# A hybrid diffusion step: the first expert weights in short runs, a third spare place, an output slot given back by TensorE

## What is computed

```python
h = rmsnorm(x, norm_mix[l]) * (1.0 + sc1) + sh1
y, new_lru, new_hgrn = token_mixer(h, ...)      # RG-LRU and HGRN2 scans, then y @ w_out
x = x + g1 * y
h = rmsnorm(x, norm_ffn[l]) * (1.0 + sc2) + sh2
x = x + g2 * expert_choice_ffn(h, w_router[l], w_gate[l], w_up[l], w_down[l])
y_out = rmsnorm(x, norm_final)
```

## Time and profile before

| | |
|---|---|
| median of 3 runs | 993.48 us (990.89 to 993.88) |
| the profiled execution | 991.45 us, span 989.7 us |
| TensorE busy | 946.9 us (96%) |
| DMA | 276.08 MB, 63.5% of the 16 engines' span on SyncE's queue |
| loads of expert pieces | 32 gate, 32 down, 30 up into the ring, 2 up into spare places |

### The profile page before, as it was taken

How to read it: one execution, slowest core, us unless ns; L and a number is a source line. 1 busy time by engine, 2 the same in 40 slices (tenths; PEclk the granted TensorE clock), 3 DMA queues, 4 the chain that set the end, 5 groups by cost and what they waited for, 6 DMA issues and landing times.

```text
span 989.7 us, 18270 instructions
## 1 busy us (share of the span) xinstructions
PE 946.9 (96%) x7806; PEld 412.4 (42%) x7806; DVE 479.7 (48%) x1136; ACT 304.4 (31%) x547; POOL 101.4 (10%) x112
## 2 busy tenths in 40 slices
PE   5999899999999999999899999999999999999996
PEld 4555556666666554463222222222222222223222
DVE  4577666464643663665445134451344415533155
ACT  5137756573653654333020020200200102002002
POOL 3200010000000011211101101011010110200100
PEclk9999999999999999999899999999999999999999
DMA  9990014504027641137899999999999999999992
GB/s 331 332 387 19 1 29 154 176 6 171 6 91 270 251 151 65 76 137 268 318 414 378 416 428 400 419 414 409 425 401 418 419 411 417 403 428 417 413 382 107
DMA packets 49828, 276.08 MB, mean 279 GB/s; under 512 B 4048, under 2 KB 12400, under 8 KB 37616
## 3 DMA queue, kind: packets, MB, share of 16 engines
q1 hardware_dynamic: 42432, 253.24, 63.5%
q0 software_dynamic: 5824, 16.81, 5.7%
q10 hardware_dynamic: 1520, 5.28, 1.4%
HBM read 262.30 MB, written 13.01 MB: 278 GB/s over the span
## 4 chain that ended last, share of the span: by engine, by line
PE 44%; DMA 7%; DVE 0%; issue 0%; ACT 0%; SPq 0%
PE p L626 26%; PE pa L626 17%; DMA ring<-in_w_down_dram 6%; PE pa L1197 0%; DMA reg_c<-h_rows,row_p 0%; DVE reg_a L2126 0%; DVE reg_a L2121 0%; ACT reg_d L1247 0%; SPq L479 0%; PE p L1091 0%; DVE reg_d L2131 0%; ACT stat L1247 0%; DVE stat L2125 0%
## 5 line engine op out<-in xcount | busy, mean ns | idle before, releaser
L626 PE MATMUL pa<-ring,reg_b 128*32 128x512 f32 (+1 forms) x2144 | 292.9, 596 | 1.0 <-ACT reg_b L1247 0.8
L626 PE MATMUL p<-ring,reg_b 128*16 128x512 f32 (+1 forms) x2528 | 280.6, 594 | 4.6 <-DMA ring<-in_w_down_dram 3.2
L626 PE MATMUL pa<-reg_a,ring 128*128 128x512 f32 (+1 forms) x768 | 227.1, 449 | 5.9 <-DVE reg_a L1624 3.3
L626 PEld LDWEIGHTS pa<-ring,reg_b 128*32 128x32 f32 (+1 forms) x2144 | 93.2, 116 | 179.8 <-issue 177.2
L626 PEld LDWEIGHTS pa<-reg_a,ring 128*128 128x128 f32 x768 | 118.1, 191 | 98.4 <-issue 98.3
L626 PEld LDWEIGHTS p<-ring,reg_b 128*16 128x16 f32 (+1 forms) x2528 | 76.6, 102 | 197.3 <-issue 196.6
L1247 ACT ACTIVATE reg_b<-pa 128x512 f32<-128x512 f32 (+1 forms) x28 | 17.1, 612 | 409.0 <-PE pa L626 213.4
L2044 DVE TENSOR_TENSOR reg_b<-reg_b,pa 128x512 f32<-128x512 f32 x16 | 11.0, 688 | 165.4 <-PE pa L626 165.1
L2028 DVE STREAM_TRANSPOSE reg_b<-reg_b 32x128 f32<-32x128 f32 x256 | 77.5, 303 | 3.8
L1247 ACT ACT_TABLE_LOAD x57 | 73.1, 1283 | 4.0 <-issue 2.8
L2028 DVE STREAM_TRANSPOSE reg_d<-reg_c 32x256 f32<-32x256 f32 x140 | 61.0, 436 | 8.7 <-DMA reg_c<-h_rows,row_s 6.7
(11 more groups left out here) (321 smaller groups left out, 750.9 us busy)
## 6 DMA issues: line engine op xcount, KB each, us to landing
ring<-in_w_gate_dram SPq DMA_DIRECT2D x32, 2048.0 KB, 12.8
ring<-in_w_down_dram SPq DMA_DIRECT2D x32, 2048.0 KB, 14.7
ring<-in_w_up_dram SPq DMA_DIRECT2D x30, 2048.0 KB, 14.1
ring<-in_w_ada_dram SPq DMA_DIRECT2D x8, 2048.0 KB
ring<-in_w_in_dram SPq DMA_DIRECT2D x6, 2048.0 KB, 20.7
ring<-in_w_ada_dram SPq DMA_DIRECT2D x8, 1024.0 KB, 12.4
ring<-in_w_out_dram SPq DMA_DIRECT2D x2, 2048.0 KB, 12.8
sum_rows<-reg_a ACTq DMA_DIRECT2D x5, 512.0 KB, 2.7
```

The source lines that it names most:

```text
L626: return nc.tensor.matmul(out, lhsT, rhs, start=start, stop=stop, **kw)
```

## The change

- u10 is loaded in four DMAs of 512 KB like u11, each partition's run being 4 KB.
- d00 gets a third spare place (`reg_e`, parts of `reg_d` and `reg_a`), loaded in four such DMAs with a semaphore of its own; SyncE waits ahead of it for the last users of these regions. d01, d10, d11 go into slots 1, 2, 3, and pair 1 begins in slot 4.
- Slot 0 (the output matrix's second half) is given back by TensorE along with slot 5, when the output sums are done.
- The prompt's g2 is loaded straight into 512 columns, the first half of the row into partitions 0 to 63, the second into 64 to 127; the copies by VectorE fall away.

```diff
-SPARE = {("u", 1, e): SLOTS for e in range(2)}
+SPARE = {("u", 1, 0): SLOTS, ("u", 1, 1): SLOTS, ("d", 0, 0): SLOTS}
...
-        g2r = g1r
+        g2r = reg_c[:, 4 * D:5 * D]
...
-        g2q = reg_e[:, 0:512]
+        g2q = reg_c[:, 5 * D:5 * D + 512]
...
+                 ("d", 0, 0): [reg_e[:, 0:D], reg_e[:, D:2 * D], reg_d[:, 2 * D:3 * D], reg_a[:, 4 * D:5 * D]]}
...
-            sp_eng.dma_start(reg_a[:, 0:4 * D].rearrange("p (k n) -> p k n", k=4), expert_rows(0, "u", 1, 0)).then_inc(loaded[SLOTS], 16)
+            for k4 in range(4):
+                sp_eng.dma_start(spare[("u", 1, 0)][k4].unsqueeze(1), expert_rows(0, "u", 1, 0)[:, k4:k4 + 1, :]).then_inc(loaded[SLOTS], 16)
...
             head_load("u", 0, 1)
-            for kh in range(2):
-                for e in range(2):
-                    head_load("d", kh, e)
+            sp_eng.wait_ge(slots_ps, 2)
+            sp_eng.wait_ge(lg_ps, NT)
+            sp_eng.wait_ge(pool_step, NT + 3)
+            sp_eng.wait_ge(ss2, NT)
+            sp_eng.wait_ge(acc_store[1], 16)
+            for k4 in range(4):
+                sp_eng.dma_start(spare[("d", 0, 0)][k4].unsqueeze(1), expert_rows(0, "d", 0, 0)[:, k4:k4 + 1, :]).then_inc(spare_down, 16)
+            head_load("d", 0, 1)
+            for e in range(2):
+                head_load("d", 1, e)
...
             pool.wait_ge(y_ps, 2 * NT)
             pool.wait_ge(g_p, 16)
-            pool.sem_inc(freed[SLOT_OF[("out", 1)][0]], 1)
...
-                    for g in range(2):
-                        pool.dma_start(g2r[g], mod_rows[2 + g].partition_broadcast(P)).then_inc(g2_in, 16)
+                    pool.dma_start(g2r, mod_rows[2].partition_broadcast(P)).then_inc(g2_in, 16)
+                    for half in range(2):
+                        pool.dma_start(g2q[64 * half:64 * half + 64, :],
+                                       mod_rows[3][512 * half:512 * half + 512].partition_broadcast(64)).then_inc(g2_in, 16)
...
             pe.wait_ge(y_ps, 2 * NT)
-            pe.sem_inc(freed[SLOT_OF[("out", 0)][0]], 1)
+            for half in range(2):
+                pe.sem_inc(freed[SLOT_OF[("out", half)][0]], 1)
...
-                                               g2r[1][rs, cols_], ALU.mult, ALU.mult)
+                                               g2q[rs, :], ALU.mult, ALU.mult)
...
-            for half in range(2):
-                rows = slice(64 * half, 64 * half + 64)
-                V.tensor_copy(g2q[rows, :], g2r[1][rows, 512 * half:512 * half + 512])
```

More of the change, by code:

```diff
@@ L264, in program @@
         hpT = reg_b[:, 3840:3840 + 512].rearrange("p (m q) -> p m q", m=4)
-        spare = [[reg_a[:, k4 * D:(k4 + 1) * D] for k4 in range(4)],
-                 [hT_p[:, :, :].rearrange("p k t -> p (k t)"), reg_b[:, 4 * D:5 * D], reg_d[:, 3 * D:4 * D], reg_c[:, 2 * D:3 * D]]]
+        spare = {("u", 1, 0): [reg_a[:, k4 * D:(k4 + 1) * D] for k4 in range(4)],
+                 ("u", 1, 1): [hT_p[:, :, :].rearrange("p k t -> p (k t)"), reg_b[:, 4 * D:5 * D], reg_d[:, 3 * D:4 * D],
+                               reg_c[:, 2 * D:3 * D]],
+                 ("d", 0, 0): [reg_e[:, 0:D], reg_e[:, D:2 * D], reg_d[:, 2 * D:3 * D], reg_a[:, 4 * D:5 * D]]}
         x_raw = reg_d[:, 0:KT * (P + 32)].rearrange("p (k n) -> p k n", k=KT)
@@ L308, in program @@
         Z_ADA, Z_CONV, Z_SCORES, Z_ROWS = 1, 2, 3, 4
-        loaded = [sem(f"ring_loaded{s}") for s in range(SLOTS)] + [sem("spare_loaded")]
+        loaded = [sem(f"ring_loaded{s}") for s in range(SLOTS)] + [sem("spare_up_loaded")]
+        spare_down = sem("spare_down_loaded")
         freed = [sem(f"ring_freed{s}") for s in range(SLOTS)] + [sem("spare_used")]
@@ L401, in weights @@
             s, _ = chunk(m, kh, e, head)
-            return wide[:, s, k4, :] if s < SLOTS else spare[e][k4]
+            return wide[:, s, k4, :] if s < SLOTS else spare[(m, kh, e)][k4]
         w_in_v = w_in[0].rearrange("(k p) n -> p k n", p=P)
@@ L469, in _ @@
                     sp_eng.wait_ge(acc_done, 2 * NT)
-                sp_eng.dma_start(spare[1][k4].unsqueeze(1), expert_rows(0, "u", 1, 1)[:, k4:k4 + 1, :]).then_inc(loaded[SLOTS], 16)
+                sp_eng.dma_start(spare[("u", 1, 1)][k4].unsqueeze(1), expert_rows(0, "u", 1, 1)[:, k4:k4 + 1, :]).then_inc(loaded[SLOTS], 16)
             head_load("u", 0, 1)
-            for kh in range(2):
-                for e in range(2):
-                    head_load("d", kh, e)
+            sp_eng.wait_ge(slots_ps, 2)
[8 more added lines that the diff above has]
+                head_load("d", 1, e)
             with sp_eng.Fori(1, PAIRS) as i:
@@ L1112, in use @@
                         s, turn = chunk(m, kh, e, head)
-                        if s == SLOTS:
-                            pe.wait_ge(loaded[s], 16 * 5)
+                        if s == SLOTS and m == "u":
+                            pe.wait_ge(loaded[s], 16 * 8)
+                        elif s == SLOTS:
+                            pe.wait_ge(spare_down, 16 * 4)
                         else:
@@ L2066, in pair_out @@
                 dve.wait_ge(out_free, i + 1)
-                dve.wait_ge(g2_in, 32)
+                dve.wait_ge(g2_in, 48)
                 for half in range(2):
@@ L2108, in sample_out @@
                 cols_ = slice(half * 512, half * 512 + 512)
-                V.tensor_tensor(out_s[:, cols_], p67[:, cols_], g2r[0][:, cols_], ALU.mult).then_inc(out_done, 1)
+                V.tensor_tensor(out_s[:, cols_], p67[:, cols_], g2r[:, cols_], ALU.mult).then_inc(out_done, 1)
             sample_out(0)
```

2 lines of the change are left out of this document (1 added, 1 removed).

## The result

The changed kernel takes 993.34 us (median of 20 runs) against 992.67 of the kernel before; the ratio is 1.0021, 95% interval 1.0013 to 1.0030. The ratio is not the quotient of the two medians: these lie 0.7 us apart, the means 1.7 us, and the ratio says 2.1 us. In all three the kernel is slower, by less than the 0.3% set as the bound of a change, and well off the forecast of 988.5. (The forecast was made against 993.48, the median of three runs.)

The account below looks back on a forecast made before the run. DMA at full rate from 523 to 958 us was the bound. Idle time 4.9 plus gate bytes 0.6 less short runs 0.3 is 5.2, less 0.2 idling: 5.0 off the 993.48 median, 988.5 us; range 986.0 to 992.5.

Parts of the forecast that it names:

- the gather's landing: Prompt's first token-row gather: issued at 467.4, taking 4.15 us or up to 0.5 more, landing at 471.5 to 472.0.
- The row store: Prompt's row store beside u10's short runs: lands in 4.2, perhaps 5 us, instead of 8.9; bounds 2.9 and 8.9.
- TensorE's side: End of the prompt's gate sums: TensorE 6.7 us earlier, 3.5 from the earlier gather plus 3.2 from the clock.
- The clock: After TensorE's wait for the prompt's gather: stays at 1.00 instead of falling to 0.50, worth 3.2 us.
- The two sides: Full DMA stretch: TensorE's side allows 6.7 us earlier, the DMA's 5.2 less 0.2 idling; the smaller decides, 5.0.
- (c): Rival: gather no sooner, the DMA's hole opens again before pair 1's u00, 1 us left: 992.5; chance 18%.
- the lead is lost there: Pair 1's u00 waits for its slot, spare place or not, so only the filled hole counts.
- the sign of being wrong: A hole of several us before pair 1's up pieces would show the forecast wrong.
- The third place: Spare place for d00: d00 follows u01 at once; only the filled DMA hole counts, no lasting lead.
- The gate columns: Prompt's second gate, before 523: 0.77 MB instead of 1.05 spread over partitions, saving 0.6 us of DMA.
- The split: u10 and d00 in four pieces each: costs 0.17 us a piece, 0.3 for both; bounds nothing and 0.6.
- (e): Rival: u01's 16 KB packets get between the prompt's gather and its end, 3.4 us slower, 996.9; chance 6%.

Follow-up runs that it names:

- short_only: The kernel before with u10 loaded in four DMAs of 4 KB runs and nothing else; 992.34 us, ratio 1.0004.
- held_again: The same program as held_till_issued in another execution, measured against the kernel before; 990.83 us, ratio 0.9988.
- held kernels: Changed kernel with weight loads u01, u11, d00 held until the prompt's gather was issued or had landed; ratios to the kernel before 1.0010, 0.9991, 0.9999 (u10 in one DMA).
- held_till_landed: The changed kernel with u01, u11 and d00 held until the prompt's gather has landed; 993.07 us, ratio 1.0010 to the kernel before.
- held_till_issued: The changed kernel with u01, u11 and d00 let go about 1 us after the prompt gather's issue; 990.98 us, ratio 0.9991 to the kernel before.
- held_full_gate: held_till_issued with the prompt's second gate loaded as whole rows into all partitions, as before; 990.09 us, ratio 0.9983 to the kernel before.
- gate_only: The kernel before with the prompt's second gate loaded as 512 columns and nothing else; 993.90 us, ratio 1.0014.
- u01_first_held: Changed kernel, u01 issued behind u00, spare pieces held for GpSimd's signal behind the prompt's gather; 993.36 us, ratio 1.0022 to the kernel before.

## Why the prediction was wrong

**The step that failed** is the gather's landing: "At 4.15 us, or up to 0.5 more as u11 still runs beside it, it lands at 471.5 to 472.0". It took 7.7. I read the 4.15 us as the price of a gather beside 4 KB packets. It was the price of a gather whose packets came as the weight queue ran dry, and the change's first part took that away. The row was there: the share from 472 to 487 was low because the queue was empty, and I counted the hole as loss alone. "Cost: one semaphore increment of TensorE, in front of nothing that waits" is the same step seen from the other side: the price was not TensorE's, it was paid by a transfer in another queue.

**The row store** is the same error again: forecast 4.2 to 5 us, measured 7.6. Turns by packets hold once packets flow; the time ahead of the first one was left out. In the kernel after, the store is issued at 463.18, and GpSimd's queue has its first packet only after 467. A term of the sum was mis-sized there, 1.3 us of gain in place of 4.3, and short_only shows that even these don't reach TensorE while weights stand ahead of the gather.

**The account of TensorE's side.** The forecast shift of the prompt turn was 3.5 us earlier, the measured one 2.3 later, 5.8 apart. The gather is 3.3 of it (7.7 against the 4.4 reckoned with). The row store is 2.5: the gather was to be issued 3.8 us earlier and was issued 1.3 earlier, each counted from the sample turn.

**The clock** was to be kept, 3.2 us; with the longer wait it wasn't. But the low stretch began during the wait (first row, no matmul in it), and ended sooner in the work:

```profile
472.87:479.37 6.50, 0.00 (x1) 0.01 (x1) 0.00 (x0) 0.00 (x0) 0.00 (x0) 0.83 1.04 395
479.37:484.04 4.67, 4.67 (x28) 1.85 (x32) 1.84 (x8) 0.00 (x0) 1.86 (x2) 0.50 0.98 403
```

In the kernel after 4.67 us of work lie in it against 6.51, which gives back 0.9 where 3.2 was forecast. With the 5.8 of the turn this makes 8.1 us between the forecast of TensorE 6.7 us early and the measured 1.4 late. So 2.3 - 0.9 = 1.4 us late at the end of the gate sums, and 1.3 at the end of the program. Even a short wait would have been no safe ground for "I take the clock as kept": after 1.54 us in held_again the clock fell (last section).

**The two sides** were right as a rule: TensorE's side is 1.4 us late, pair 1's up pieces are issued late by it, and the DMA idles in front of them (0.57), as (c) and "the lead is lost there" said; it is also the hole that was named as the sign of being wrong. The held kernels show the other side: with TensorE early, its waits in the pairs grow, as forecast.

**The third place** was forecast to count by the filled hole. In the changed kernel it seems to, 1.7 us; with TensorE early or with the gather as before, nothing clear of noise. **The gate columns** were to give 0.6 us, and no run shows it. **The split** of u10 was priced at 0.17 us a piece, and short_only (1.0004, end 535.3 against 535.2) is in line with a price that small. The 2 us for each DMA in the anatomy section of the Trainium skill's "DMA: Bandwidth & Descriptors", which describes DMAs issued from GpSimd, didn't show in SyncE's filled queue.

**The rival (e)** was the nearest in its mechanism, with 6%: u01's loads get between the gather and its end, 3.6 us of gather instead of 4.4. Its condition was not met as it stood: the row store landed at 470.8, but in a trace that runs 1.6 us later, so 1.3 us earlier than before when counted from the sample turn. Its reason was only partly right: the packets' length is 0.9 of it, and a full queue the rest. Its price was not met either: 3.4 us slower was said, 996.9. Of the 3.6 the earlier store took off 1.3 and the clock 0.9, and (c)'s gain of 1 us from the filled hole did not come. The 8.6 us from which it took its 4.4 are moreover those of a gather of 128 rows, not of 32; that its size came out near is partly luck.

**What stays open.** The ratio says 2.1 us, the profiled executions 1.3 behind the sample turn. Whether the falls of the clock before 150 us, which differ from trace to trace, are more common in some kernels isn't known. Why the DMA is slower while 64 partitions are written wasn't tried.

## What to carry to other kernels

Before a hole in the DMA is filled, ask which small transfer on the critical path is served in it: its time in the trace may be that of a queue that was just running empty. A small transfer that must be quick is issued ahead of bulk loads, and these are let go a moment behind it (1 us was enough here); when TensorE and DMA are nearly level, count both sides, since the smaller gain decides.

## What the runs showed of the hardware

- A gather issued 0.1 us behind bulk loads, with an idle DMA, took 6.5 us; with the loads 1 us behind it, 2.8 to 3.0; with a full queue ahead, 6.5 to 8.3. The Trainium skill, "DMA: Bandwidth & Descriptors", section "Queues, rings and completion order", says that a DMA engine takes turns between its queues by packets. The shares of the earlier trace rows agree once packets flow; the 2.4 us without one packet of the second queue are not in that rule.
- After a wait of TensorE of 1.79 us in held_till_landed the granted clock was 0.50 for part of the next 5.1 us (mean 0.67), and after one of 1.54 in held_again too (mean 0.70 over 5.68 us). After one of 1.81 in held_till_issued and one of 1.93 in held_full_gate it stayed at 1.00. These are the window of held_till_landed, then that of held_again:

```profile
475.88:481.00 5.12, 5.12 (x36) 1.76 (x40) 1.85 (x8) 0.60 (x1) 1.86 (x2) 0.67 0.83 298
```

```profile
474.32:480.00 5.68, 5.68 (x40) 1.78 (x44) 1.84 (x8) 0.60 (x1) 1.86 (x2) 0.70 0.91 377
```

- In the 5 us from 515 to 520, with the gate loads into 64 partitions each under way beside the weights (gate_only), the DMA moved 333 GB/s at a share of 1.00; in the kernel before, with whole rows into all partitions, 423 at 1.02.
- In u01_first_held, a semaphore that GpSimd raises behind an indirect DMA had let SyncE's next load go before that DMA was issued (472.54 against 472.65 in the trace).
